# A two-layer decoder trunk on one core: small loads moved to ScalarE's queue, chunk 0's weights placed among the modulation loads, and the work ahead of the first layer put in another order

## The reference, cut to what matters

```python
mod = (c_act @ ada_w[l] + ada_b[l])[:, None, :]           # c_act = silu(c); (D, 6*D) weights
sh1, sc1, gt1, sh2, sc2, gt2 = jnp.split(mod, N_MOD, axis=-1)
h = rms_norm(x, norm1_g[l]) * (1.0 + sc1) + sh1
x = x + gt1 * token_mixer(h, ...)      # three branches from h @ w_in, merged, then @ w_o
h = rms_norm(x, norm2_g[l]) * (1.0 + sc2) + sh2
x = x + gt2 * conv_gated_mlp(h, ...)   # h @ w_up, causal conv, silu gate, @ w_down
```

## Time and profile before

| what | value |
|---|---|
| three runs | 1060.69, 1061.27, 1066.18 us (median 1061.27) |
| profiled execution | 1060.32 us, its span 1058.5 us |
| PE busy | 999.8 us of the span (94%) |
| DVE, ACT, POOL busy | 749.2, 523.5, 17.9 us |
| moved by DMA | 201.25 MB, mean 190 GB/s |
| first product of layer 0's first chunk | 46.63 us after the span's start |

### The profile page before, as it was taken

How to read it: one execution, slowest core, us unless ns; L and a number is a source line. 1 busy time by engine, 2 the same in 40 slices (tenths; PEclk the granted TensorE clock), 3 DMA queues, 4 the chain that set the end, 5 groups by cost and what they waited for, 6 DMA issues and landing times.

```text
span 1058.5 us, 20502 instructions
## 1 busy us (share of the span) xinstructions
PE 999.8 (94%) x7837; PEld 919.9 (87%) x7837; DVE 749.2 (71%) x1127; ACT 523.5 (49%) x733; POOL 17.9 (2%) x23
## 2 busy tenths in 40 slices
PE   4699999989999999999999999998999999999997
PEld 2498888888988999989898998887988989999997
DVE  2448789995485788876335688999657678878743
ACT  2545355647344655654345544555653456555532
POOL 5000000000000000000000000000000000000001
PEclk9899999999999999999999999999999999999998
DMA  8765445536695355966763545345667635555451
GB/s 309 277 199 176 155 141 170 175 107 200 238 325 192 120 188 171 332 242 246 279 199 97 155 124 169 122 160 180 194 207 277 239 120 184 174 166 193 162 198 41
DMA packets 138952, 201.25 MB, mean 190 GB/s; under 512 B 3416, under 2 KB 114148, under 8 KB 138852
## 3 DMA queue, kind: packets, MB, share of 16 engines
q1 hardware_dynamic: 138501, 199.63, 56.4%
q10 hardware_dynamic: 351, 0.26, 0.1%
HBM read 198.83 MB, written 1.05 MB: 189 GB/s over the span
## 4 chain that ended last, share of the span: by engine, by line
PE 72%; DVE 13%; issue 9%; DMA 2%; ACT 2%; SPq 2%; DVEq 0%; ACTq 0%
PE PB L1276 16%; PE PB L1278 15%; PE PB L1277 15%; DVE wL L864 3%; DVE buf L947 3%; PE MI L1227 2%; PE SC L1276 2%; PE SC L1278 2%; PE SC L1277 2%; DMA raw<-in_w_in 2%; DVE rdev L1005 1%; PE PB L1299 1%; PE ST L1329 1%; DVE cb L1093 1%; PE SC L1392 1%
## 5 line engine op out<-in xcount | busy, mean ns | idle before, releaser
L864 DVE TENSOR_TENSOR wL<-raw,wH 128x2048 fp32r<-128x2048 f32 (+3 forms) x152 | 320.7, 2112 | 117.9 <-ACT wH L608 116.0
L1276 PE MATMUL PB<-hH,wH 128*128 128x256 f32 x1376 | 399.0, 290 | 4.9 <-DVE wL L864 4.8
L1277 PE MATMUL PB<-hL,wH 128*128 128x256 f32 x1376 | 389.1, 283 | 0.0
L1278 PE MATMUL PB<-hH,wL 128*128 128x256 f32 x1376 | 389.0, 283 | 0.0
L608 ACT ACTIVATE wH<-raw 128x2048 fp32r<-128x2048 f32 (+3 forms) x152 | 266.5, 1770 | 121.4 <-DMA raw<-in_w_down 56.3
L1276 PEld LDWEIGHTS PB<-hH,wH 128*128 128x128 f32 x1376 | 262.9, 191 | 25.7 <-issue 15.8
L1277 PEld LDWEIGHTS PB<-hL,wH 128*128 128x128 f32 x1376 | 263.1, 191 | 2.2 <-issue 1.7
L1278 PEld LDWEIGHTS PB<-hH,wL 128*128 128x128 f32 x1376 | 263.1, 191 | 0.0
L947 DVE SCALAR_TENSOR_TENSOR buf<-G,vec,buf 128x256 f32<-128x256 f32 x240 | 98.0, 477 | 0.3
L1299 PE MATMUL PB<-hH,wH 128*128 128x256 f32 x192 | 57.0, 297 | 15.7 <-DVE hL L881 12.8
L1093 DVE SCALAR_TENSOR_TENSOR cb<-PB,vec,cb 128x255 f32<-128x255 f32 (+1 forms) x88 | 36.4, 475 | 32.2 <-ACT cb L755 32.2
(11 more groups left out here) (257 smaller groups left out, 1727.7 us busy)
## 6 DMA issues: line engine op xcount, KB each, us to landing
raw<-in_w_in SPq DMA_DIRECT2D x48, 1024.0 KB, 5.4
raw<-in_w_up SPq DMA_DIRECT2D x44, 1024.0 KB, 5.1
ada<-in_ada_w SPq DMA_DIRECT2D x40, 1024.0 KB, 7.2
raw<-in_w_down SPq DMA_DIRECT2D x22, 1024.0 KB, 4.9
ada_pre<-in_ada_w SPq DMA_DIRECT2D x8, 1024.0 KB, 11.3
raw<-in_w_o SPq DMA_DIRECT2D x8, 1024.0 KB, 8.2
raw<-in_w_out_diff SPq DMA_DIRECT2D x4, 1024.0 KB, 5.1
raw<-in_w_out_conv SPq DMA_DIRECT2D x4, 1024.0 KB, 7.5
```

Of the source, the lines that this page charges most:

```text
L864: dve.tensor_tensor(wL[s][:, 0:size], raw[s][:, 0:size], wH[s][:, 0:size].bitcast(F32), ALU.subtract).then_inc(w_lo[s], 1)
L1276: pe.matmul(out, a, xh(k), start=first and k == 0, stop=False, skip_group_check=True)
L1277: pe.matmul(out, a, xl(k), start=False, stop=False, skip_group_check=True)
L1278: ins = pe.matmul(out, b, xh(k), start=False, stop=last and k == kt - 1, skip_group_check=True)
```

## The change

1. SP keeps only large loads: x, then the eight `ada_pre` loads, with chunk 0's weights issued after the fifth. The positions go to ACT's queue behind `cst`, all 13 vectors follow `final_g` there, then `diff_lambda` and the mask.
2. ACT rounds chunk 0 (`high(0, 0)`) after `root(0, 0)` and makes the rotary tables behind it, between the two modulation evictions; before, the tables came first. The first eight `hH` tiles are interleaved with chunk 1's rounding in four quarters.
3. DVE does `flush_vectors(0)`, the reciprocal (`invert`) and `low(0, 0)` before the second modulation part is ready, and only `scale_now` and `scaled` after it. `low(0, 1)` follows.
4. In the loop, what opened an iteration now closes the one before it: DVE's `flush_vectors`, `scale_now` and `norm` of layer 1, ACT's `shifted` and SP's load of chunk 0 stand in the `If` at the end of layer 0's iteration.
5. POOL makes the angles first (waiting for x to be turned, and using `xn` as scratch in place of `rdev`) and the mask's bf16 copy and `identb` after them; PE waits for these only at its first scores.

```diff
@@ SP, ahead of the loop
-            sp.dma_start(pos_i[:, :], positions.broadcast_to([P, T])).then_inc(s_pos, 16)
-            sp.dma_start(mask[:, :], consts[:, C_MASK:NC_CONST]).then_inc(s_mask, 16)
-            sp.dma_start(lam_in[:, :, :, :]..., diff_lambda...).then_inc(s_lam, 16)
             for a in range(ADA_FIRST):
-                load_vectors(sp, vectors[1 + 4 * a:5 + 4 * a] if a in (1, 2) else [])
+                if a == ADA_PART + 1:
+                    load(0, 0)
                 part, i = divmod(a, ADA_PART)
                 sp.dma_start(ada_pre[:, a, :, :], ...)
@@ SP, the loop
             with sp.Fori(0, LAYERS) as l:
-                for n in range(UP):
+                for n in range(1, UP):
...
+                with sp.If(l < LAYERS - 1):
+                    load(l + 1, 0, layer=LAYERS - 1)
@@ POOL
-            pool.wait_ge(s_mask, 16)
-            pool.tensor_copy(maskb[:, :], mask[:, :])
-            pool.tensor_copy(identb[:, :], ident).then_inc(s_const, 1)
             pool.wait_ge(s_pos, 16)
+            pool.wait_ge(s_xtr, 4)
...
+            pool.wait_ge(s_mask, 16)
+            pool.tensor_copy(maskb[:, :], mask[:, :])
+            pool.tensor_copy(identb[:, :], ident).then_inc(s_const, 1)
@@ ACT, its DMA issues
             act.dma_start(cst[:, :], consts[:, 0:C_MASK]).then_inc(s_cst, 16)
+            act.dma_start(pos_i[:, :], positions.broadcast_to([P, T])).then_inc(s_pos, 16)
             act.dma_start(rows[DT:2 * DT, 8, :], final_g...).then_inc(s_cvec, 16)
-            load_vectors(act, vectors[0:5])
+            load_vectors(act, vectors)
+            act.dma_start(lam_in[:, :, :, :]..., diff_lambda...).then_inc(s_lam, 16)
+            act.dma_start(mask[:, :], consts[:, C_MASK:NC_CONST]).then_inc(s_mask, 16)
@@ ACT, ahead of the loop
             squares(0, 0)
-            act.wait_ge(s_ang, 1)
-            act.wait_ge(s_ones, 1)
-            act.activation(turns[:, :, :], ang[:, :, :], ACT.Abs).then_inc(s_abs, 1)
-            act.activation(sin[:, :, :], ang[:, :, :], ACT.Sin)
-            act.wait_ge(s_abs, 1)
-            act.activation(cos[:, :, :], turns[:, :, :], ACT.Sin, ...).then_inc(s_table, 1)
...
+            act.wait_ge(s_ones, 1)
             ada_evict(ADA_PART)
             root(0, 0)
+            high(0, 0)
+            act.wait_ge(s_ang, 1)
+            act.activation(turns[:, :, :], ang[:, :, :], ACT.Abs).then_inc(s_abs, 1)
+            act.activation(sin[:, :, :], ang[:, :, :], ACT.Sin)
+            act.wait_ge(s_abs, 1)
+            act.activation(cos[:, :, :], turns[:, :, :], ACT.Sin, ...).then_inc(s_table, 1)
             ada_evict(2 * ADA_PART)
-            high(0, 0)
-            high(0, 1)
+            shifted(0, 0, 0, 2)
+            act.wait_ge(raw_in[1], 16)
+            for q in range(4):
+                part = slice(q * SLOT // 4, (q + 1) * SLOT // 4)
+                ins = act.activation(wH[1][:, part], raw[1][:, part], ACT.Copy)
+                if q < 3:
+                    shifted(0, 0, 2 + 2 * q, 4 + 2 * q)
+            ins.then_inc(w_hi, 1)
             with act.Fori(0, LAYERS) as l:
-                shifted(l, 0)
...
                 with act.If(l < LAYERS - 1):
                     squares(l + 1, 0)
                     root(l + 1, 0)
+                    shifted(l + 1, 0)
@@ DVE, ahead of the loop
-            dve.wait_ge(s_vt, 1 + LAYERS)
-            ada_end(0, 1, vec_all[:, 0, :])
...
+            dve.wait_ge(s_vt, 1 + LAYERS)
+            flush_vectors(0)
+            ada_end(0, 1, vec_all[:, 0, :])
+            invert(0, 0)
+            low(0, 0)
             dve.wait_ge(s_table, 1)
-            low(0, 0)
             ada_end(1, 2, vec_all[:, 0, :])
+            scale_now(0)
+            scaled(0, 0)
+            low(0, 1)
@@ DVE, the loop
             with dve.Fori(0, LAYERS) as l:
-                flush_vectors(l)
-                norm(l, 0)
-                with dve.If(l < 1):
-                    low(l, 1)
...
                 with dve.If(l < LAYERS - 1):
                     low(l + 1, 1)
+                    flush_vectors(LAYERS - 1)
+                    scale_now(l + 1)
+                    norm(l + 1, 0)
@@ PE
-            after(s_const, 1)
...
+                    if use == "D0":
+                        after(s_const, 1)
```

More of the change, by code:

```diff
@@ L416, in _, with load @@
             ada_v = ada_w.rearrange("l (k p) c -> p (l k) c", p=P)
-            def load(l, n, r=0):
+            def load(l, n, r=0, layer=None):
                 s = n % RAW
@@ L432, in load @@
                 if n < LAT + 2:
-                    src = in_v[l, :, :, n * 256:(n + 1) * 256]
+                    src = in_v[l if layer is None else layer, :, :, n * 256:(n + 1) * 256]
                 elif n == LAT + 2:
@@ L477, in _ @@
                          x[0, :, :].rearrange("(a p) d -> p a d", p=P)).then_inc(s_x, 16)
-            sp.dma_start(pos_i[:, :], positions.broadcast_to([P, T])).then_inc(s_pos, 16)
-            sp.dma_start(mask[:, :], consts[:, C_MASK:NC_CONST]).then_inc(s_mask, 16)
-            sp.dma_start(lam_in[:, :, :, :].rearrange("p l a b -> p (l a b)"),
-                         diff_lambda.rearrange("(o l) a b -> o (l a b)", o=1).broadcast_to([P, LAYERS * 4 * HD])).then_inc(s_lam, 16)
             for a in range(ADA_FIRST):
-                load_vectors(sp, vectors[1 + 4 * a:5 + 4 * a] if a in (1, 2) else [])
+                if a == ADA_PART + 1:
+                    load(0, 0)
                 part, i = divmod(a, ADA_PART)
@@ L536, in _ @@
             for part in (TWO_PI_1, TWO_PI_2, TWO_PI_3):
-                link(pool.tensor_scalar(rdev[:, :], flat2(turns), -part, None, ALU.mult))
-                link(pool.tensor_tensor(flat2(ang), flat2(ang), rdev[:, :], ALU.add))
+                spare = xn[:, 0:2, :]
+                link(pool.tensor_scalar(spare, turns[:, :, :], -part, None, ALU.mult))
+                link(pool.tensor_tensor(ang[:, :, :], ang[:, :, :], spare, ALU.add))
             edge = float(np.nextafter(np.float32(math.pi), np.float32(0)))
             pool.tensor_scalar(ang[:, :, :], ang[:, :, :], edge, -edge, ALU.min, ALU.max).then_inc(s_ang, 1)
+            pool.wait_ge(s_mask, 16)
+            pool.tensor_copy(maskb[:, :], mask[:, :])
+            pool.tensor_copy(identb[:, :], ident).then_inc(s_const, 1)
             pool.wait_ge(sq_ready, LAYERS * 2 * DT + 1)
@@ L555, in _ @@
             act.dma_start(cst[:, :], consts[:, 0:C_MASK]).then_inc(s_cst, 16)
+            act.dma_start(pos_i[:, :], positions.broadcast_to([P, T])).then_inc(s_pos, 16)
             act.dma_start(rows[DT:2 * DT, 8, :], final_g.rearrange("(k p) -> k p", p=P)).then_inc(s_cvec, 16)
-            load_vectors(act, vectors[0:5])
+            load_vectors(act, vectors)
+            act.dma_start(lam_in[:, :, :, :].rearrange("p l a b -> p (l a b)"),
+                          diff_lambda.rearrange("(o l) a b -> o (l a b)", o=1).broadcast_to([P, LAYERS * 4 * HD])).then_inc(s_lam, 16)
+            act.dma_start(mask[:, :], consts[:, C_MASK:NC_CONST]).then_inc(s_mask, 16)
             act.wait_ge(s_vt, 1)
@@ L595, in _ @@
             squares(0, 0)
-            act.wait_ge(s_ang, 1)
-            act.wait_ge(s_ones, 1)
-            act.activation(turns[:, :, :], ang[:, :, :], ACT.Abs).then_inc(s_abs, 1)
-            act.activation(sin[:, :, :], ang[:, :, :], ACT.Sin)
-            act.wait_ge(s_abs, 1)
-            act.activation(cos[:, :, :], turns[:, :, :], ACT.Sin, bias=half_pi[:, :], scale=-1.0).then_inc(s_table, 1)
             def high(l, n, r=0):
@@ L624, in root, with shifted @@
                 act.activation(touch[:, :], eps[:, :], ACT.Tanh).then_inc(touched, 1)
-            def shifted(l, which):
-                for k in range(DT):
+            def shifted(l, which, first=0, last=DT):
+                for k in range(first, last):
                     act.wait_ge(xn_ready, l * 2 * DT + which * DT + k + 1)
@@ L764, in up_step @@
                                    gy[:, :, :].rearrange("p k t -> p (k t)"), ACT.Copy).then_inc(g_hi, 1)
+            act.wait_ge(s_ones, 1)
             ada_evict(ADA_PART)
             root(0, 0)
-            ada_evict(2 * ADA_PART)
-            high(0, 0)
-            high(0, 1)
+            high(0, 0)
[3 more added lines that the diff above has]
+            act.wait_ge(s_abs, 1)
+            act.activation(cos[:, :, :], turns[:, :, :], ACT.Sin, bias=half_pi[:, :], scale=-1.0).then_inc(s_table, 1)
+            ada_evict(2 * ADA_PART)
+            shifted(0, 0, 0, 2)
[6 more added lines that the diff above has]
+            ins.then_inc(w_hi, 1)
             with act.Fori(0, LAYERS) as l:
-                shifted(l, 0)
                 for n in range(WO):
@@ L870, in norm, with invert, scaled @@
             def norm(l, which):
+                invert(l, which)
+                scaled(l, which)
+            def invert(l, which):
                 dve.wait_ge(st_read, FREE + l * len(ST_USES) + (1, 7)[which])
```

(8 more changed lines are left out.)

## The result

| | before | after |
|---|---|---|
| median, 20 runs of each | 1063.17 us | 1066.42 us |
| lowest | 1060.28 us | 1064.50 us |
| profiled execution (span) | 1060.32 (1058.5) us | 1065.11 (1062.9) us |
| start of the vectors' turning (V) | 19.62 us | 28.12 us |
| first product of layer 0 | 46.63 us | 50.05 us |

The change made the kernel slower by a quarter of a per cent: ratio 1.0026, 95% interval 1.0015 to 1.0037. The forecast was 0.14% faster. By the bound set with it (0.5%) this is no change; 20 runs of each tell the sign all the same. The median of before is 1.9 us above that of the first three runs; the 1228.32 us of one execution of the changed kernel, at a mean clock of 0.757, is left out of the ratio.

The account below looks back on a forecast made before the run. The prediction took PE's feeding as the bound, at the start and between the layers. It summed +1.8 us at the start and -3.25 between the layers to -1.45: 1059.8 us on the 1061.27 median, range 1053 to 1067.

Parts of the forecast that it names:

- V: At the start, the time all 13 vectors have landed: 26 us taken, range 23.3 to 30, 19.6 before.
- The load path: At the start, the last `ada_pre` load lands at 36.9 and the first `xn` starts about 40.2, 4.7 us earlier.
- the idle share: DMA engines' idle time between 7 and 10 us, filled by larger loads: 0.29 x 3.0 = 0.9 us off the last landing.
- From V to the first xn: At the start, products, `norm_sum` and ACT's work ahead of the second eviction put the first `xn` at V + 20.7.
- The part that needs nothing opposite: In V, terms besides waiting on SP's packets: start at 2.8 us, 140 small packets of 0.021, 15 transfers at 0.25 each.
- The turns: In V, ACT's small packets alternate one for one with SP's: 80 waits of 0.153 us and 51 of 0.050, 14.8.
- spare turns: In V, turns against chunk 0's packets were to cover 2 us of the cost of 15 transfers.
- Between the layers: At the passage to layer 1, DVE's copies follow `low` at once, gaining 1.85 us; 3.25 with the clock, bounds 1.85 to 3.55.
- the clock: In layer 1's first products, PE's granted clock stays at 1.00 after less idle time: 1.4 us gained.
- Early vectors: Rival at the start: V falls to 19.5 or less, the loads bind, the start gains 4.7 us; 1053.4 us, chance 0.30.
- Very late vectors: Rival at the start: held-up SP issues hold up ACT's, V near 33, `xn` 8.8 us later; 1066.9 us, chance 0.18.
- Nothing between the layers: Rival: DVE's wait belongs to the `If` or the copies and moves along with them; 1063.1 us, chance 0.10.

Follow-up runs that it names:

- vectors_back: The changed kernel with the last eight vectors issued by SP between the first `ada_pre` loads again; 1058.63 us, ratio 0.9960 to the kernel before.
- tables_first: The changed kernel with the rotary tables back ahead of ACT's first eviction; 1063.60 us, ratio 1.0006 to the kernel before.
- rows_split: The changed kernel with the load of conv_dw_w's 124 rows cut into 112 and 12; 1062.13 us, ratio 0.9989 to the kernel before.
- loop_only: The kernel before with only the loop turned, layer 1's opening work closing layer 0's iteration, SP's loads as before; 1061.15 us, ratio 0.9978.
- queue_only: The kernel before with all its small loads moved to ACT's queue and nothing else; 1087.83 us, ratio 1.0218.
- after_again: The changed kernel as it stands, executed once more; 1065.74 us, ratio 1.0019 to the kernel before.
- after_third: The changed kernel as it stands, a third profiled execution; 1063.24 us.

## Why the prediction was wrong, point by point

**The load path: right in kind, its gain too large.** With V out of the way (vectors_back) the loads bind and the whole kernel is faster by 0.4%. But the last `ada_pre` load lands at 37.80 and the first `xn` starts at 41.95, where 36.9 and 40.2 were predicted: 3.0 us gained, not 4.7. The load lands where chunk 0 did (37.75), so in this run nothing was had from the idle share. Another 0.8 is the reduction, 1.87 us at the lower clock for the 1.05 of the earlier trace rows. This path doesn't bind in the changed kernel, so its error isn't in the 2.6 us.

**From V to the first xn: right.** V + 20.7 was predicted, V + 20.2 measured, with the second eviction behind ACT's own order. tables_first shows what the tables cost on the path, 2.8 us (their work was 3.1 in the sum).

**V: this is the step that failed at the start, by its size.** The mechanism, one packet of ACT's for one of SP's, fits every run: 11.59 with nothing opposite but x, 23.04 with half packets, 24.83 with fewer rows on the slowest engines, 33.71 with no short packets opposite. The size was off: 28.12, not 26, inside the bounds of 23.3 to 30 but 2.1 us above the value taken. The 26 doesn't follow from its own terms either: 23.3 + 15 x 0.25 - 2 is 25.0, and with 0.35 and 0.5 it is 26.5 and 28.8 in place of 27.6 and 30, so they were 3.1 us short. The part that needs nothing opposite was right: 2.8 + 2.4 for x + 2.9 + 3.8 = 11.9, and 11.59 measured. The turns were not: 14.8 us in the prediction, 28.12 - 11.59 = 16.5 measured, 1.7 too few, and the 2 us of transfers that spare turns were to cover don't show. The 140 small packets of the slowest engine had been read off a 3 us lag, where rows_split shows that the shape of one single load, 124 rows, puts 46 packets too many there. That this accounts for the whole 1.7 is argued, not shown: no view gives packets by engine. The first `xn` was at 48.32 in place of 46.7, the first product +3.41 in place of +1.8.

**Between the layers: mechanism right, gain too large.** DVE's gap went from the path, as foretold, the reciprocal came 1.1 us behind `low` and the clock stayed at 1.00. But the gain up to layer 1's first product was 1.1 us (from +3.78 to +2.68), not 1.85. The step that failed here is the overlap: the prediction let PE start as soon as `hL` was ready, and PE started 1.0 us later (562.01 and 562.99). Most of the other 1.5 us (to +1.12) is the clock. It was forecast as 1.4 and the first trace gives it, but the second trace of before has no low clock there either: against it the turned loop gives 1.26 us (3.56 at the end of layer 0, 2.30 at 650 us), 0.4 of them behind the first product. loop_only gives 1.2 by the same comparison. So the 1.4 was taken in full for something that three of four executions had, and that came back elsewhere: the number of stretches a trace didn't fall.

**Sum.** Without the stretches of low clock the prediction amounts to +1.8 - 1.85, nothing; measured is +2.6 in the traces and +3.3 in the medians. Of the 2.6, the start missed 1.6, layer 0 added 0.4 (from +3.41 to +3.78), and the turned loop fell short by 0.6. With the clock's 1.4 this is the way from -1.45 to +2.6. V alone doesn't account for the sign: with V right, the change would still have cost 1.0. What is left between 2.6 and 3.3 isn't placed; how often either kernel meets the stretches could make it, and three executions each don't tell.

**The rivals.** Early vectors are refuted by V: 16.5 us of waiting were measured. The prediction had tied them to the Trainium skill's rule (DMA: Bandwidth & Descriptors, Queues, rings and completion order), by which an engine drains a packet of some 9 to 17 descriptors from one ring before it turns to the next. That rule doesn't make them early: if both rings give as many at a turn, small and large rows still pass one for one on average. Only longer turns for ACT's ring than for SP's would, and these the measured wait rules out; how many go at a turn no run here shows. Very late vectors (32.8 and more) didn't come about here, but queue_only with 33.71 shows how near they were: chunk 0's place among the loads is what kept them away. ACT's issues were held up too, for 7.93 us; as that went with the split of conv_dw_w, ACT's own queue is the likely cause, and not SP's. *Nothing between the layers* is refuted by loop_only.

## What to carry to other kernels

In these runs a queue beside a busy one got about one packet for each of the neighbour's, whatever their sizes: rows of 512 bytes opposite rows of 4 KB moved at the pace of the latter, and an empty queue for small loads was no fast lane. If they must share, send them first, cut the large load's rows, or keep them in order in one queue, and look at the number of rows on the slowest engine, not at the bytes. A price taken from a stretch of low clock in one trace should be read in further traces of the same kernel before it is put in a sum. And where a wait is taken off one engine, look what the others do at the same point: the next one to hold the path may have a like gap.

## What the runs showed that was not expected

- The kernel before had, behind its start, one stretch of 3.4 us at the granted clock of 0.5 (1.2 GHz) in two executions (1060.3 and 1060.8 us) and four in a third (1065.6 us). All lie just behind idle time of PE, but the idle time alone doesn't decide: ahead of 743 us PE was busy 1.33 of 3.40 us in both of these executions of the changed kernel, and the clock fell in after_again (first fence) and stayed up in after_third (second). What decides was not found.

```profile
739.80:743.20 3.40, 1.33 (x8) 0.82 (x7) 3.40 (x9) 1.41 (x1) 0.00 (x0) 1.00 0.20 62
743.20:748.20 5.00, 5.00 (x22) 4.35 (x23) 3.59 (x9) 1.72 (x8) 0.00 (x0) 0.66 0.00 0
```

```profile
739.80:743.20 3.40, 1.33 (x8) 0.83 (x6) 3.40 (x9) 1.29 (x1) 0.00 (x0) 1.00 0.14 47
```

- The number of rows in a small load matters by its divisors: 124 rows cut to 112 and 12 took 3.3 us off V.
- At the place of the jump back, DVE was idle for 1.92 us before and ACT for 2.19 us after, and ACT loaded a table (1.28 us at 568.31) for a plain copy behind it.
